# A mixture-of-experts kernel: the first expert pair gathered feature by feature in fp32 between its first steps, and one weight slot filled earlier

## What is computed

```python
def expert_choice_moe(h, w_router, w_gate, w_up, w_down):
    cap = max(1, CAPACITY_FACTOR * s // N_EXPERTS)          # 64 tokens for each of 16 experts
    aff = jax.nn.softmax((h @ w_router).astype(jnp.float32), axis=-1)
    gates, idx = lax.top_k(jnp.swapaxes(aff, 1, 2), cap)
    xg = jax.vmap(lambda hb, ib: hb[ib])(h, idx)
    a = jax.nn.silu(jnp.einsum("becd,edf->becf", xg, w_gate)) * jnp.einsum("becd,edf->becf", xg, w_up)
    yo = jnp.einsum("becf,efd->becd", a, w_down) * gates[..., None].astype(h.dtype)
    return jax.vmap(lambda ib, vb: jnp.zeros((s, d), vb.dtype).at[ib.reshape(-1)].add(vb.reshape(-1, d)))(idx, yo)
```

## Time and profile before

| | |
|---|---|
| median of three runs | 1876.35 us (1876.14 to 1881.18) |
| span of the profiled execution | 1877.1 us |
| its own time | the profile gives none beside the span |
| PE busy | 1831.2 us (98%) |
| PE weight loads | 1365.5 us (73%) |
| DVE busy | 1007.7 us (54%) |
| ACT busy | 631.1 us (34%) |
| moved from memory | 321.25 MB read |

### The profile page before, as it was taken

How to read it: one execution, slowest core, us unless ns; L and a number is a source line. 1 busy time by engine, 2 the same in 40 slices (tenths; PEclk the granted TensorE clock), 3 DMA queues, 4 the chain that set the end, 5 groups by cost and what they waited for, 6 DMA issues and landing times.

```text
span 1877.1 us, 23248 instructions
## 1 busy us (share of the span) xinstructions
PE 1831.2 (98%) x9860; PEld 1365.5 (73%) x9860; DVE 1007.7 (54%) x1472; ACT 631.1 (34%) x921; POOL 0.2 (0%) x4
## 2 busy tenths in 40 slices
PE   7999999999999999999999999999999999999998
PEld 6788777788887886343443443797888779988998
DVE  6654366633565643222212322756766799777775
ACT  5322245433243421211112111444442345343331
POOL 0000000000000000000000000000000000000000
PEclk9999999999999999999999999999999999999999
DMA  6223211032244327999999999323221223323231
GB/s 188 90 90 94 86 51 37 24 116 90 90 135 135 109 116 314 428 427 427 429 427 427 427 428 417 116 75 90 83 74 46 90 68 113 112 91 110 92 113 46
DMA packets 136007, 324.85 MB, mean 173 GB/s; under 512 B 7504, under 2 KB 118368, under 8 KB 122464
## 3 DMA queue, kind: packets, MB, share of 16 engines
q1 hardware_dynamic: 135760, 322.32, 46.2%
q10 hardware_dynamic: 144, 1.05, 0.1%
HBM read 321.25 MB, written 2.10 MB: 172 GB/s over the span
## 4 chain that ended last, share of the span: by engine, by line
PE 83%; DMA 8%; DVE 5%; ACT 2%; issue 1%; SPq 0%; DVEq 0%; ACTq 0%
PE bank L636 20%; PE bank L637 19%; PE bank L638 19%; PE bank L1124 12%; DMA ew_b<-in_w_exp_up 2%; DMA ew_f<-in_w_exp_up 2%; DMA ew_g<-in_w_exp_up 2%; DMA ew_c<-in_w_exp_up 2%; PE bank L1148 2%; PE bank L835 2%; PE bank L1083 1%; PE bank L1324 1%; DVE w_lo L2156 1%; ACT w_hi L1606 1%; DMA raw<-in_w_in 1%
## 5 line engine op out<-in xcount | busy, mean ns | idle before, releaser
L636 PE MATMUL bank<-H_hi,w_hi 128*128 128x512 f32 (+2 forms) x992 | 375.8, 379 | 3.4 <-DVE H_lo L2156 1.8
L637 PE MATMUL bank<-H_lo,w_hi 128*128 128x512 f32 (+2 forms) x992 | 371.0, 374 | 0.0
L638 PE MATMUL bank<-H_hi,w_lo 128*128 128x512 f32 (+2 forms) x992 | 370.9, 374 | 0.0
L2156 DVE TENSOR_TENSOR w_lo<-raw,w_hi 128x2048 fp32r<-128x2048 f32 (+2 forms) x110 | 209.8, 1920 | 186.0 <-ACT w_hi L1606 173.0
L636 PEld LDWEIGHTS bank<-H_hi,w_hi 128*128 128x128 f32 x992 | 186.9, 188 | 47.2 <-issue 8.4
L638 PEld LDWEIGHTS bank<-H_hi,w_lo 128*128 128x128 f32 x992 | 186.9, 188 | 36.1
L637 PEld LDWEIGHTS bank<-H_lo,w_hi 128*128 128x128 f32 x992 | 186.9, 188 | 35.1 <-issue 0.7
L1606 ACT ACTIVATE w_hi<-raw 128x2048 fp32r<-128x2048 f32 x74 | 141.2, 1908 | 128.0 <-PE bank L638 120.4
L2568 DVE SCALAR_TENSOR_TENSOR SG<-bank,gs,SG 128x512 f32<-128x512 f32 x16 | 11.3, 746 | 206.6 <-PE bank L1124 206.6
L636 PE MATMUL bank<-C_hi,w_hi 128*128 128x512 f32 x160 | 65.9, 412 | 4.8 <-DVE C_lo L2209 4.7
L638 PE MATMUL bank<-C_hi,w_lo 128*128 128x512 f32 x160 | 64.6, 404 | 0.0
(11 more groups left out here) (586 smaller groups left out, 3877.9 us busy)
## 6 DMA issues: line engine op xcount, KB each, us to landing
raw<-in_w_in SPq DMA_DIRECT2D x36, 1024.0 KB, 5.5
raw<-in_w_ff SPq DMA_DIRECT2D x32, 1024.0 KB, 5.5
ew_b<-in_w_exp_up SPq DMA_DIRECT2D x8, 2048.0 KB, 27.4
ew_c<-in_w_exp_gate SPq DMA_DIRECT2D x8, 2048.0 KB, 27.0
ew_c<-in_w_exp_up SPq DMA_DIRECT2D x6, 2048.0 KB, 30.6
ew_b<-in_w_exp_gate SPq DMA_DIRECT2D x6, 2048.0 KB, 23.9
raw<-in_w_mem_kv SPq DMA_DIRECT2D x8, 1024.0 KB, 5.4
ew_d<-in_w_exp_up SPq DMA_DIRECT2D x4, 2048.0 KB, 26.1
```

Of the source, the lines that this page charges most:

```text
L636: pe.matmul(o, lhs[0], rhs[0], start=first, stop=False, **kw)
L637: pe.matmul(o, lhs[0], rhs[1], start=False, stop=False, **kw)
L638: return pe.matmul(o, lhs[1], rhs[0], start=False, stop=last, **kw)
L2156: return dve.tensor_tensor(out=dst, in0=src, in1=hi_part.bitcast(F32), op=ALU.subtract)
```

## The change

The first pair is no longer gathered token by token and transposed. For each q, eight fp32 matmuls with a 128 x 128 part of TK (every fourth column) as the weights and 128 columns of OH produce the feature-major tiles 2q and 2q + 1 directly, and ACT copies them to XG. These four groups stand just ahead of the four gate steps. T0_hi and T0_lo are no longer made. The filler matmuls read TK in fp32, 13, 1 and 1 of them. Load 9 is issued with loads 2 and 3. Some semaphores are merged without a change in what they order.

```diff
-BUSY = 48
+BUSY = 13
...
-        T0_hi = place("T0_hi", [P, TT, S], F32R, R + 48 * K)
-        T0_lo = place("T0_lo", [P, TT, S], F32R, R + 56 * K)
...
+        def first_bank(q):
+            return (bank[4], bank[5], bank[2], bank[3])[q]
...
-                    o = tile((tk_ready if at + j >= 4 else chunk_lo_ready, at + j + 1))
+                    o = tile((tk_ready, at + j + 1))
...
-            pe.wait_ge(chunk_hi_ready, 4)
+            pe.wait_ge(tk_ready, 4)
...
-                    pe.matmul(bank[5][:, :], T0_hi[:, i % TT, 0:P], T0_hi[:, i % TT, :], start=True, stop=True)
+                    pe.matmul(bank[5][:, :], TK[:, i % TT, 0:P], TK[:, i % TT, 0:S], start=True, stop=True)
...
-            busy(2)
+            busy(1)
...
-            busy(4)
+            busy(1)
...
-            def first_gather():
-
-                pe.wait_ge(oh_ready, 1)
-                pe.wait_ge(chunk_lo_ready, 4)
-                for tt in range(TT):
-                    for part in (T0_hi, T0_lo):
-                        ins = pe.matmul(bank[4][:, :], OH[:, tt, :], part[:, tt, :],
-                                        start=(tt == 0 and part is T0_hi), stop=(tt == TT - 1 and part is T0_lo))
-                mark(ins, ("first", 0))
-                for tt in range(TT):
-                    ins = pe.matmul(bank[5][:, :], OH[:, tt, :].bitcast(F32), TK[:, tt, S:2 * S],
-                                    start=(tt == 0), stop=(tt == TT - 1))
-                mark(ins, ("first", 1))
+            def first_gather(q):
+
+                o = marks.tile = first_bank(q)
+                for j in range(2):
+                    half, i = divmod(2 * q + j, 4)
+                    for tt in range(TT):
+                        ins = pe.matmul(o[:, j * P:(j + 1) * P], TK[:, tt, half * S + i:(half + 1) * S:4],
+                                        OH[:, tt, :].bitcast(F32), start=(tt == 0), stop=(tt == TT - 1))
+                mark(ins, ("first", q))
...
             pe.wait_ge(pos_ready, 1)
-            first_gather()
-            for half in range(2):
-                feature_turn(0, half)
+            pe.wait_ge(oh_ready, 1)
             for p in range(EPAIRS):
                 if p:
                     pe.wait_ge(at_ready, 2 * p)
                 for q in range(4):
-                    pe.wait_ge(xg_ready, 2 * p + q // 2 + 1)
+                    if p == 0:
+                        first_gather(q)
+                    pe.wait_ge(xg_ready, 4 + 2 * (p - 1) + q // 2 + 1 if p else q + 1)
                     expert_step(p, 0, q, XG, gate_banks(p))
...
-                    if n < 4:
-                        act.activation(T0_hi[:, n, :], o[:, :], ACT.Copy).then_inc(chunk_hi_ready, 1)
...
-            for half in range(2):
-                done(act, ("first", half))
-                act.activation(SG[:, half * S:(half + 1) * S], bank[4 + half][:, :], ACT.Copy).then_inc(xt_ready, 1)
-            featured(0)
+            for q in range(4):
+                done(act, ("first", q))
+                act.activation(XG[:, 2 * q:2 * q + 2, :], first_bank(q)[:, 0:2 * P].rearrange("p (a b) -> p a b", a=2),
+                               ACT.Copy).then_inc(xg_ready, 1)
...
-                    if m == 6:
-                        for n in range(4):
-                            dve.wait_ge(chunk_hi_ready, n + 1)
-                            rest(T0_lo[:, n, :], marks.banks[("tk", n)][:, :], T0_hi[:, n, :]).then_inc(chunk_lo_ready, 1)
...
             def one_hot(p):
 
                 if p:
-                    done(dve, ("ot", p - 1))
+                    done(dve, ("ot", p - 1) if p > 1 else ("first", 3))
...
-            for g in (2, 3):
+            for g in (2, 3, 9):
                 expert_load(g, 0, 2)
...
             done(sp, ("tk", 7))
             expert_load(8, 0, 2)
-            done(sp, ("first", 0))
-            expert_load(9, 0, 2)
```

More of the change, by code:

```diff
@@ L381, in build @@
         x_ready = sem("x_ready")
[L382 to L386, removed]
+        meta_act_ready = sem("meta_act_ready")
+        meta_dve_ready = sem("meta_dve_ready")
         meta2_ready = sem("meta2_ready")
@@ L672, in _ @@
             pe.wait_ge(consts_in, 16 * N_CONST)
-            pe.wait_ge(meta_sq_ready, 1)
+            pe.wait_ge(meta_act_ready, 1)
             for k in range(KT):
@@ L703, in _ @@
                     pe.wait_ge(lat_sq_ready, 3)
-                    pe.wait_ge(meta_std_ready, 1)
+                    pe.wait_ge(meta_act_ready, 2)
                     mark(pe.matmul(bank[5][:, :], ones[:, :], sq[:, 2, :], start=True, stop=True), "ss_kv")
@@ L1080, in gather @@
                         pe.wait_ge(x_ready, 8 * (p - 2) + 16 + 4 + half + 1)
-                    pe.wait_ge(chunk_lo_ready, 4 + 8 * (p - 1) + c + 1)
+                    pe.wait_ge(chunk_lo_ready, 8 * (p - 1) + c + 1)
                     for part in (chunk_hi, chunk_lo):
@@ L1085, in gather @@
                     mark(ins, ("gather", p, c))
-            def first_gather():
-                pe.wait_ge(oh_ready, 1)
-                pe.wait_ge(chunk_lo_ready, 4)
-                for tt in range(TT):
-                    for part in (T0_hi, T0_lo):
-                        ins = pe.matmul(bank[4][:, :], OH[:, tt, :], part[:, tt, :],
-                                        start=(tt == 0 and part is T0_hi), stop=(tt == TT - 1 and part is T0_lo))
-                mark(ins, ("first", 0))
-                for tt in range(TT):
-                    ins = pe.matmul(bank[5][:, :], OH[:, tt, :].bitcast(F32), TK[:, tt, S:2 * S],
-                                    start=(tt == 0), stop=(tt == TT - 1))
-                mark(ins, ("first", 1))
+            def first_gather(q):
[6 more added lines that the diff above has]
+                mark(ins, ("first", q))
             def feature_turn(p, half):
-                pe.wait_ge(xt_ready, 2 * p + half + 1)
+                pe.wait_ge(xt_ready, 2 * (p - 1) + half + 1)
                 for i in range(4):
@@ L1630, in _ @@
             act.wait_ge(consts_in, 16 * N_CONST)
-            act.activation(meta_sq[:, :, :], meta[:, :, :], ACT.Square).then_inc(meta_sq_ready, 1)
+            act.activation(meta_sq[:, :, :], meta[:, :, :], ACT.Square).then_inc(meta_act_ready, 1)
             for m in range(KT):
@@ L1644, in _ @@
                     act.activation(meta_sq[:, 0, :], bank[5][:, 0:META], ACT.Sqrt, bias=eps, scale=1.0 / D)\
-                       .then_inc(meta_std_ready, 1)
+                       .then_inc(meta_act_ready, 1)
                 if m == 5:
@@ L1651, in _ @@
             his("mix1")
-            act.wait_ge(meta_n_ready, 1)
-            act.activation(meta_hi[:, :, :], meta[:, :, :], ACT.Copy).then_inc(meta_hi_ready, 1)
+            act.wait_ge(meta_dve_ready, 1)
+            act.activation(meta_hi[:, :, :], meta[:, :, :], ACT.Copy).then_inc(meta_act_ready, 1)
             split_hi(U0["lat"] + 3)
@@ L1914, in meta_copies @@
                 act.activation(los[:, :, 0:META], meta_lo[:, :, :].bitcast(F32), ACT.Copy).then_inc(meta2_ready, 1)
-            act.wait_ge(meta_lo_ready, 1)
+            act.wait_ge(meta_dve_ready, 2)
             meta_copies(U_hi, U_lo)
@@ L2226, in _ @@
             latent(3, kr[:, :])
-            dve.wait_ge(meta_std_ready, 1)
+            dve.wait_ge(meta_act_ready, 2)
             link(dve.reciprocal(meta_sq[:, 0, :], meta_sq[:, 0, :]))
@@ L2233, in _ @@
                               in1=meta_sq[:, 0, :].unsqueeze(1).broadcast_to([P, KT, META]), op=ALU.mult)\
-               .then_inc(meta_n_ready, 1)
-            dve.wait_ge(meta_hi_ready, 1)
-            rest(meta_lo[:, :, :], meta[:, :, :], meta_hi[:, :, :]).then_inc(meta_lo_ready, 1)
+               .then_inc(meta_dve_ready, 1)
+            dve.wait_ge(meta_act_ready, 3)
+            rest(meta_lo[:, :, :], meta[:, :, :], meta_hi[:, :, :]).then_inc(meta_dve_ready, 1)
             dve.wait_ge(edges_set, 1)
@@ L2554, in chunks @@
                     half, tt = divmod(c, TT)
-                    dve.wait_ge(chunk_hi_ready, 4 + 8 * (p - 1) + c + 1)
+                    dve.wait_ge(chunk_hi_ready, 8 * (p - 1) + c + 1)
                     rest(chunk_lo[c % 3][:, :], TK[:, tt, half * S:(half + 1) * S], chunk_hi[c % 3][:, :])\
```

## The result

The changed kernel is slower. Over 16 runs each, its median is 1890.8 us (1884.27 to 1896.31) against 1881.03 us (1875.1 to 1885.61) for the kernel before. The ratio is 1.0051 with a 95% interval of 1.0038 to 1.0065, some 9.6 us. The forecast was +3 us, 1879.3 us, in a range that ended at 1884.5 us. It started from three runs of the kernel before with a median of 1876.35 us; over 16 runs that kernel's median is 4.7 us higher. So 4.7 of the 11.5 us between forecast and result are the starting level. The change's own part, 1.0051 times 1876.35 us, would be 1885.9 us, still beyond the range. The span of the profiled execution is 1889.6 us against 1877.1.

A forecast was written before the change was run, and what follows sets the result against it. The expert weight load stream was taken as the bound. PE's delay, 10.9 + 1.0 - 7.6 - 0.6 = 3.7 us, less 0.6 is 3.1; span 1877.1 + 3.0 = 1880.1, median 0.75 below: 1879.3 us, range 1873 to 1884.5.

The forecast's parts named there:

- delay less 0.6 us: Expert weight stream: if PE ends step (0, 0, 3) later by X, the stream ends later by X - 0.6 us.
- The pauses: Weight stream in the first pair: expected idle ahead of load 10's second halves, 12, 12's second halves and 14.
- I take 0.12: The 64 first-pair gather instructions: 0.12 us apart, so 16 per round take 1.92 us.
- upper bound of 0.18: Gather instruction spacing at most 0.111 + 0.069 = 0.18 us, if the strided load's whole extra length shows; 3.8 us more.
- Rival 1: The 64 gather instructions: strided weight loads are serial, 0.18 us each, end 6.6 us later at 1883; chance 0.17.
- the prediction's sum: PE up to step (0, 0, 3): X = 10.9 + 1.0 - 7.6 - 0.6 = 3.7 us later.
- the half clock that did not come: Gather instructions from about 730.4 to 733.8 us: some 11 take 0.21 us at 1.2 GHz, adding 1.0 us.
- the earlier start: PE starts the first gather 0.6 us earlier than 732.1 us, from the bank stall and filler changes.
- The wait for XG: End of each of four gather rounds: PE waits 0.7 us for ACT's copy, bounds 0.65 to 1.0 with 0.1 us return.
- The stall at L636: PE's 0.68 us stall on the bank disappears, a gain of 0.68 us for everything behind.
- The early load 9: Load 9 moves to about 654 us; its 4.91 us leave the saturated stretch, a gain only if the stream stays full.
- Rivals 3 and 4: 3: gather rounds shorter than thought, 1872 to 1876 us, chance 0.15. 4: pauses hidden, unchanged 1876, chance 0.05.

The follow-up runs named there:

- two delay kernels: Kernel before plus ten fp32 matmuls (8.6 us) after step (0, 0, 2) or (3, 0, 2): 1889.6 and 1875.5 us; last weight wait 443.6 and 435.3 us after load 8.
- step 1: Changed kernel with first-pair gathers reading 128 neighbouring TK columns instead of every fourth: 1882.6 us instead of 1889.6, last weight wait 438.6 us after load 8 instead of 445.9.
- one group ahead: Changed kernel with each gather group one step ahead: load 12's second halves 48.8 us after load 8 instead of 51.4, last weight wait 444.3 us.
- step 8: Changed kernel with gathers reading every eighth TK column instead of every fourth: last weight wait 446.5 us after load 8's issue, against 445.9.
- ordered kernel: Changed kernel with TK's features put in gather order by ACT's copies, so gathers read neighbouring columns: ratio 1.0007 (0.9993 to 1.0021) to the kernel before.
- fourth-pair delay: Kernel before with ten extra fp32 matmuls (8.6 us) on PE after step (3, 0, 2): 1875.5 us beside 1875.2; last weight wait 435.3 us after load 8.
- ordered version one ahead: The ordered kernel with each gather group one step ahead: ratio 1.0011 (0.9998 to 1.0024) to the kernel before.

## Why the prediction was wrong

**The bound and the way to the end: right.** The stream of expert weights carries the first pair's delay to the end. The sum said delay less 0.6 us; the two delay kernels gave 8.9 and 8.3. In the change, load 12's second halves are 8.3 us later in absolute time and the last weight wait 6.8, which is less 1.5; with both kernels at full clock in the first gather it is 11.4 and 10.6, less 0.8. So the rule holds and its constant is known only to about 1 us. The pauses stand where they were forecast. Load 8 itself comes 0.9 us earlier than before, counted from loads 2 and 3; 10.6 less 0.9 is 9.7 us, and the runs gave 9.6.

**The step that failed** is the price of a gather instruction, "I take 0.12", and with it its upper bound of 0.18. It measured 0.232. Over 64 instructions that is over 7 us. The neighbouring columns of step 1 gave 0.111, just as in the earlier trace rows. The 0.117 us came from transposes with the same step, which load once each; a plain fp32 matmul's loads, with the same step, start twice as far apart. The prediction said that the rows bear on transposes only, and still took the transposes' spacing as the likeliest. Its upper bound was 0.111 us plus the 69 ns by which a strided transpose load is longer. Adding the extra length was nearly right: at step 4 it is 137 ns for these loads, and the spacing grows by 121. But 69 ns is the transpose's figure, and the rule on 16-byte lines that the prediction cited beside it gives no price; that it meant this bound was the prediction's own step. The trace before had a sign that the two kinds differ: with neighbouring columns, the loads of plain fp32 matmuls (L835, L1097) are listed at 190 to 192 ns, those of transposes at 141. Rival 1 had the right place and direction, at 3.8 us instead of 7, and with a chance of 0.17. Its name says more than was found: loads of 0.33 us that start 0.232 us apart still overlap.

Put into the prediction's sum, what was measured closes it. 3.7 us, plus 64 x (0.235 - 0.12) = 7.4 for the instructions, less 1.0 for the half clock that did not come and 1.5 for the earlier start (both below), is 8.6 us, against the 8.3 measured.

**Terms that held.** The wait for XG measured 0.66 us against 0.7, and one group ahead brought 2.5 us in SP's issues against 2.0. The stall at L636 is gone. The early load 9 gained nothing, as the sum had it. Rivals 3 and 4 did not happen.

**Terms that missed, in small.** PE began to gather 2.1 us earlier instead of 0.6 (730.0 against 732.1). Of this, 1.1 us was there when loads 2 and 3 were issued, 652.06 against 653.2 us, and is not the change's: in the step 8 and the ordered kernel, which have the change, they were issued at 653.2. The 1.0 us for half clock in the gather did not come: PEclk is 1.00 throughout 728 to 735 us. Half clock came elsewhere, after the last weight wait and around 1450 us, where the profiled spans gained another 5.7 us of difference.

**What stays open.** Why the clock falls to half around 1450 us in some executions and not in others was not tried. It did so in the profiles of ten of the 13 kernels, but not in that of the kernel before, of the fourth-pair delay (tail 725.5 us), or of step 8, which has the change (725.4). The unprofiled runs show no sign that the change moves how often it happens. In both kernels 4 of the 16 times form a low group, 1875.1 to 1876.4 us before and 1884.3 to 1884.8 us after, and the other 12 begin at 1880.4 and 1888.2. The low groups lie 8.6 us apart and the high ones 9.6, so the loss is there at either level. For the small differences between the versions it matters more: 10 of the 29 runs of the kernel before had a mean granted clock of 0.995 or more, but 7 of 12 of the ordered version and only 1 of 12 of the ordered version one ahead. Among runs with that clock, the ordered version's median is 1879.2 us against 1876.1 us for the kernel before. At 0.992 or less it is 1884.0 against 1882.6 us. So the ordered version is probably 1 to 3 us slower than the kernel before; this grouping was made after the fact.

## What to carry to other kernels

Weights of a plain fp32 matmul should lie together: here, loads with a step of four columns came half as fast as loads of neighbours, and writing the tile in the right order, in a copy that was made anyway, cost nothing. Where a stream of loads bounds a stage, look for the moment at which its queue is nearly empty. In the first pair, a delay of the compute engine that frees the buffers counted almost one for one; in the fourth, with loads queued ahead, the same delay cost nothing. A load issued earlier gained nothing here, because in its old place it held no other load up. A price for an operation in a form that the trace does not show should not be taken from a relative: the transposes had the same step, but neither the length nor the spacing of the matmul's loads.

## What the runs showed of the hardware

- fp32 weight loads of 128 x 128 in two-pass matmuls start 0.111, 0.119, 0.176, 0.232 and 0.236 us apart at column steps of 1, 2, 3, 4 and 8 (full clock), and are listed at 192, 197, 261, 329 and 335 ns.
- Loads for transposes, with a step of 4, are listed at 210 ns instead of 141 and start 0.117 us apart instead of 0.12.
- ACT copies 128 x 512 from PSUM in 597 ns when it reads every fourth column, as fast as in order.
- Runs of one kernel spread by over 10 us, with the mean granted clock: the changed kernel took 1884.3 to 1884.8 us in four of five runs at 0.995 or 0.996, and 1889.4 to 1896.3 us in the eleven at 0.991 to 0.993. In the profiles a tail that is 4.4 to 8 us longer goes with half clock for about 10 us around 1450 us. A median of three runs does not settle which level it stands for.
